# A two-block transformer kernel: order of work at the stage borders, more places for squares, weight loads exchanged, tiles joined

## The reference

```python
for l in range(DEPTH):                       # DEPTH = 2
    h = rms_norm(x, ln_mix[l])
    x = x + parallel_mixer(h, ...)           # grouped attention (g) beside latent attention (m), 8 heads each
    h = rms_norm(x, ln_mem[l])
    x = x + memory_cross_attention(h, rms_norm(mem, ln_mem_kv[l]), ...)
    h = rms_norm(x, ln_ffn[l])
    x = x + expert_choice_moe(h, ...)        # 16 experts, 64 tokens each, width 512
return rms_norm(x, ln_final)
```

```python
c_q  = rms_norm(q_lat, mla_q_norm);  q_m = (c_q @ w_q_b)
c_kv = rms_norm(kv_lat[..., :128], mla_kv_norm);  kv = (c_kv @ w_kv_b)
```

## Time and profile before

| | |
|---|---|
| median of three runs | 3210.32 us |
| the profiled execution | 3204.61 us |
| its span in the trace | 3202.8 us |
| PE busy | 2946.7 us (92%) |
| DVE, ACT, POOL busy | 1430.5, 1154.4, 264.8 us |
| mean DMA rate | 129 GB/s, in the expert stages 418 to 419 |
| mean granted clock of TensorE | 0.962 of full speed |

### The profile page before, as it was taken

The page is one execution under the profiler, slowest core; times in us unless marked ns, Lnnn a source line. Parts: engine busy times, 40 slices in busy tenths (PEclk is TensorE's granted clock), DMA queues, the critical chain, the costliest instruction groups (busy, mean ns, idle before and its releaser), DMA issues. The chain is left out here.

```text
span 3202.8 us, 41642 instructions
## 1 busy us (share of the span) xinstructions
PE 2946.7 (92%) x16852; PEld 2194.3 (69%) x16852; DVE 1430.5 (45%) x2193; ACT 1154.4 (36%) x1929; POOL 264.8 (8%) x350
## 2 busy tenths in 40 slices
PE   7999979978999899988999879999999899879998
PEld 5657855436668755446778658887887688658886
DVE  5665432246565423234544663322324553654444
ACT  4554421123654411143143542223223333543332
POOL 0011010000001200011012310000001012200000
PEclk9999989989999899989999989999999999989999
DMA  3011239961002379953332002323321132012221
GB/s 147 27 40 64 96 159 419 418 278 60 15 29 105 118 311 412 419 218 126 131 101 79 15 27 92 132 105 119 118 79 42 69 117 92 14 53 97 100 92 40
DMA packets 61356, 414.31 MB, mean 129 GB/s; under 512 B 6976, under 2 KB 7360, under 8 KB 13552
## 3 DMA queue, kind: packets, MB, share of 16 engines
q1 hardware_dynamic: 55520, 392.59, 31.4%
q0 software_dynamic: 4496, 16.98, 1.7%
q10 hardware_dynamic: 1152, 2.10, 0.2%
HBM read 409.53 MB, written 2.10 MB: 129 GB/s over the span
## 5 line engine op out<-in xcount | busy, mean ns | idle before, releaser
L1533 ACT ACTIVATE arena<-banks 128x512 f32<-128x512 f32 (+4 forms) x522 | 291.2, 561 | 933.8 <-PE banks L785 811.8
L785 PE MATMUL banks<-weight,arena 128*64 128x512 f32 (+5 forms) x2264 | 464.1, 570 | 44.6 <-ACT arena L1533 18.1
L785 PE MATMUL banks<-hidden,weight_part 128*128 128x512 f32 (+1 forms) x2304 | 446.3, 355 | 0.0
L785 PE MATMUL banks<-tokens_high,weight_part 128*128 128x512 f32 (+1 forms) x1536 | 420.5, 359 | 22.4 <-DVE tokens_low L2183 22.1
L785 PEld LDWEIGHTS banks<-hidden,weight_part 128*128 128x128 f32 x2304 | 381.0, 189 | 70.3 <-DVE arena L2183 3.5
L2287 DVE TENSOR_TENSOR weight_part<-weight,weight_part 128x2048 fp32r<-128x2048 f32 x124 | 285.4, 2305 | 224.1 <-ACT weight_part L1533 223.9
L1533 ACT ACTIVATE weight_part<-weight 128x2048 fp32r<-128x2048 f32 x124 | 236.6, 1909 | 370.7 <-PE banks L785 348.6
L785 PEld LDWEIGHTS banks<-weight,arena 128*64 128x64 f32 (+2 forms) x2264 | 165.1, 135 | 294.7 <-issue 251.6
L785 PEld LDWEIGHTS banks<-tokens_high,weight_part 128*128 128x128 f32 x1536 | 276.5, 191 | 81.3 <-DVE tokens_low L2183 28.7
L785 PE MATMUL banks<-tokens_low,weight_part 128*128 128x512 f32 (+1 forms) x768 | 274.6, 358 | 0.0
L2926 POOL TENSOR_TENSOR arena<-arena 128x512 f32<-128x512 f32 x72 | 88.7, 1232 | 1889.3 <-ACT arena L1533 1039.9
(11 more groups left out here) (217 smaller groups left out, 4137.5 us busy)
## 6 DMA issues: line engine op xcount, KB each, us to landing
weight<-in_w_gate SPq DMA_DIRECT2D x64, 1024.0 KB, 13.6
weight<-in_w_up SPq DMA_DIRECT2D x64, 1024.0 KB, 8.1
weight<-in_w_down SPq DMA_DIRECT2D x64, 1024.0 KB, 11.3
weight<-in_w_ff SPq DMA_DIRECT2D x64, 1024.0 KB, 4.8
weight<-in_ada_w SPq DMA_DIRECT2D x48, 1024.0 KB, 6.6
weight<-in_w_in SPq DMA_DIRECT2D x28, 1024.0 KB, 4.8
weight<-in_w_o SPq DMA_DIRECT2D x8, 1024.0 KB, 4.8
weight<-in_w_mem_kv SPq DMA_DIRECT2D x8, 1024.0 KB, 4.8
```

What stands on the lines that cost most here:

```text
L785: mm = lambda o, a, b, first=True, last=True: eng.matmul(o, a, b, start=first, stop=last, skip_group_check=True)
L1533: act = lambda o, i, f=ACT.Copy, **k: eng.activation(o, i, f, **k)
```

## The change

1. **Mixer, both layers.** The projections ckv and kr and both small norms' sums move from ahead of the attention into its turns 1 and 2. The four products for V of the latent branch move from turns 2 to 5 to turns 4 to 7, the splits of w_o two or three turns on.
2. **Squares.** For the entry of the mixer of layer 1 and of the block, `SQW` gives eight places for squares that lie in tensors not in use then, and `SQC` eight for the context. The last scatter runs without sums between its tiles; `entry_sums` takes them behind it, POOL's part last but one.
3. **Order in the experts' last pair.** The split of the mixer's first weight goes ahead of the last expert outputs' rounding on ACT and DVE. In layer 1 three ada chunks stand before the scatter, three behind it, two behind the sums, and the context's sums (before: ahead of the scatter) are put around the turn of the ada rows.
4. **ada.** The stationary operand has 32 columns (two conditions and zeros) instead of 2, all four groups of rows are written, and ACT copies the whole bank once instead of two rows four times. In the feed-forward of layer 0 `ada_rows` goes one chunk earlier.
5. **Loads.** In the block of layer 0 the ada chunks go one to three places ahead in SP's list against w_sv, w_nq, w_nk and w_nv.
6. **Feed-forward.** The split of the first ff1 chunk moves to the end of the stage before. Its first two tiles are joined (`joint3`); in layer 0 two more token tiles follow, then the context's first two joined, then two more. DVE makes all eight h, then all eight low parts, instead of alternating.
7. **Block layer 1.** ACT's work for the context (`block_high`, `context_shift`) goes behind its copies of the uv tiles.

The core of the diff:

```diff
@@ loads of block layer 0
             cols("w_u", 1024)
+            conditioned(1, AHEAD, AHEAD + 1)
             cols("w_sv", 1280)
-            conditioned(1, AHEAD, AHEAD + 3)
+            conditioned(1, AHEAD + 1, AHEAD + 4)
             outs(0)
-            conditioned(1, AHEAD + 3, KD)
+            conditioned(1, AHEAD + 4, KD)
+            conditioned(2, 0, 1)
             cols("w_nq", 256)
-            conditioned(2, 0, 2)
+            conditioned(2, 1, 3)
             cols("w_nk", 512)
...
@@ PE, ada
-                    i = mm(o[32 * g:32 * g + 2, :], CS[:, k, :], w[:, 512 * g:512 * g + 512], k == 0, k == KD - 1)
+                    i = mm(o[32 * g:32 * g + 32, :], CS[:, k, :], w[:, 512 * g:512 * g + 512], k == 0, k == KD - 1)
@@ PE, end of the experts
                 if l:
-                    norm_sums(("n1c", 0), NS, range(KD), KD, "one1024", CT)
+                    for k in range(3):
+                        ada(0, 0, k, PO)
                 scatter(PAIRS - 1)
-                norm_sums(nxt, NS, range(KD - 2, KD), KD, "one1024")
+                if l:
+                    for k in range(3, 6):
+                        ada(0, 0, k, PO)
+                entry_sums(nxt, NS)
@@ PE, entry of the block
-                    for k in range(KD):
+                    for k in range(6, KD):
                         ada(0, 0, k, PO)
+                    norm_sums(("n1c", 0), S, range(2), KD, "one1024", CT)
                     ada_turn(0, 0, PB)
+                    norm_sums(("n1c", 0), S, range(2, KD), KD, "one1024", CT)
@@ PE, turns of the mixer's attention
+                    if i == 1:
+                        norm_sums(("cq", l), S, range(2), 2, "one256")
+                        w = wcur[0] = weight_parts(("w_in", l, 4))
+                        tile3(("ckv", l), halves(w, 0), HP)
+                    if i == 2:
+                        norm_sums(("ckv", l), S, range(1), 1, "one128")
+                        tile3(("kr", l), halves(wcur[0], 1), HP, free=(WF(("w_in", l, 4)),))
@@ PE, first ff1 chunks
+                        if i == 0:
+                            first = wh, wl
+                            joint3([("f1", l, 0, m) for m in ms], [halves(first, m) for m in ms], XP, ...)
+                            continue
+                        for m in ms:
+                            tile3(("f1", l, 0, m), halves((wh, wl), m % 2), XP, ...)
+                        if both:
+                            joint3([("f1c", l, 0, m) for m in range(2)], [halves(first, m) for m in range(2)], CP, ...)
@@ ACT
+                if not both:
+                    block_high(l, S, 1)
+                    context_shift(l, S)
...
-                for g in range(4):
-                    act(AD[32 * g:32 * g + 2, :], ring.get(("ada", l, q))[32 * g:32 * g + 2, :]).then_inc(...)
+                act(AD, ring.get(("ada", l, q))).then_inc(*done(("ad", l, q), ring.free(("ada", l, q))))
@@ DVE, mod_norm
-                        if n == 2 and k >= 2:
-                            eng.wait_ge(*after(("hh", tag, k - 2)))
-                            stt(parts["HL"][:, k - 2, cols], H[:, k - 2, cols], ...)
+                    for k in range(KD if n == 2 else 0):
+                        eng.wait_ge(*after(("hh", tag, k)))
+                        stt(parts["HL"][:, k, cols], H[:, k, cols], ...)
```

More of the change, by code:

```diff
@@ L600, in build @@
             b = dict(H=(Carve(0) if l else c)(KD, T), HNH=c.rounded(f"rows_high{l}", TB, D))
+            b["SQW"] = Ring(st, "SQW" + t, [Carve(c.at - (KD - k) * T)(T) for k in range(KD)])
             low_at = c.at
@@ L1510, in _ @@
                                       [(S["HH"][:, k, cols], S["HL"][:, k, cols]) for k in range(KD)], N,
-                                      free=(WF(key),) if m % 2 and part == parts[-1][0] else (),
-                                      needs=[("h2", (tag, l), k) for k in range(KD)] if (s, m) == (0, 0) else ())
+                                      free=(WF(key),) if m % 2 and part == parts[-1][0] else ())
                     else:
@@ L1667, in _ @@
                 squares(("cq", l), S, [PB.get(("cq", l, j)) for j in range(2)])
-                eng.wait_ge(*after(("out", ("ckv", l))))
-                squares(("ckv", l), S, [PB.get(("ckv", l))])
-                root(("cq", l), S)
-                root(("ckv", l), S)
                 high(4)
-                copy(S["KR"][64:128, :], ("kr", l), PB.get(("kr", l))[64:128, :], ("krc", l))
                 def mla_prep(h):
@@ L1695, in mix_between @@
                 def mix_between(i):
-                    if 2 <= i < 2 + TB:
-                        copy(S["VM"][:, i - 2, :], ("vm", l, i - 2), PB.get(("vm", l, i - 2)))
+                    if i == 1:
+                        root(("cq", l), S)
+                        eng.wait_ge(*after(("out", ("ckv", l))))
+                        squares(("ckv", l), S, [PB.get(("ckv", l))])
+                    if i == 2:
+                        root(("ckv", l), S)
+                        copy(S["KR"][64:128, :], ("kr", l), PB.get(("kr", l))[64:128, :], ("krc", l))
+                    if VM_AT <= i < VM_AT + TB:
+                        copy(S["VM"][:, i - VM_AT, :], ("vm", l, i - VM_AT), PB.get(("vm", l, i - VM_AT)))
                     if i in PREP_AT:
@@ L1819, in _ @@
                         eng.wait_ge(*after(("scattered", l, p - 1)))
+                    if p == PAIRS - 1 and l == 0:
+                        split_high(("w_in", 1, 0))
+                    if p == PAIRS - 1 and l:
+                        for other in meet("block2"):
+                            eng.wait_ge(*other)
+                        eng.wait_ge(*after(("ctx",)))
+                        squares(("n1c", 0), B["four", 0], [C[:, k, :] for k in range(KD)], n=CT)
                     for ch in range(2):
@@ L1830, in _ @@
                 exp_set()
-                if l == 0:
-                    split_high(("w_in", 1, 0))
                 S4 = B["four", 0]
                 if l:
-                    for other in meet("block2"):
-                        eng.wait_ge(*other)
-                    eng.wait_ge(*after(("ctx",)))
-                    squares(("n1c", 0), S4, [C[:, k, :] for k in range(KD)], n=CT)
                     eng.wait_ge(*after(("final_scale",)))
@@ L2375, in mix_between @@
                 def mix_between(i):
+                    if i == 1:
+                        apply(("cq", l), S, [PB.get(("cq", l, j)) for j in range(2)], [S["CQ"][:, j, :] for j in range(2)], lambda k: v1("mla_q", l, k),
+                              lambda k: (("cqn", l),) if k else (), frees=[(PB.free(("cq", l, j)),) for j in range(2)])
+                    if i == 2:
+                        apply(("ckv", l), S, [PB.get(("ckv", l))], [S["CKV"]], lambda k: v1("mla_kv", l), lambda k: (("ckvn", l),),
+                              frees=[(PB.free(("ckv", l)),)])
+                    if i == 4:
+                        eng.wait_ge(*after(("krc", l)))
+                        tt(S["TBB"][R, :], K[E, :], S["TAB"][E, 3, :], MUL).then_inc(*done())
+                        tt(K[R, :], K[R, :], S["TAB"][R, 2, :], MUL).then_inc(*done())
+                        eng.wait_ge(vector_step, done.count)
+                        tt(K[R, :], K[R, :], S["TBB"][R, :], ADD).then_inc(*done(("ks", l)))
+                        eng.wait_ge(vector_step, done.count)
                     if i - 1 in PREP_AT:
@@ L2495, in expert_low @@
                 def expert_low(p):
+                    if p == PAIRS - 1 and l == 0:
+                        split_low(("w_in", 1, 0))
                     for ch in range(2):
```

199 lines of the change are left out of this document (108 added, 91 removed).

## The result

The changed kernel takes 3132.25 us at the median of four runs (3127.12 to 3141.26) against 3210.96 (3210.0 to 3211.62, four runs): the medians lie 78.7 us apart; by the ratio, 0.9765 with a 95% interval of 0.9751 to 0.9778, it is some 2.4% faster. The forecast was 3129 in a range of 3104 to 3164. Run again later, the same kernel gave 3137.32 at the median of four (ratio 0.9777, 0.9763 to 0.9790): executions of one program lie up to 14 us apart here (3127.12 to 3141.26), and that spread has a part in what follows.

A forecast was written before the change was run, and what follows sets the result against it. PE was taken as the bound, busy 2946.7 of 3202.8 us, with the whole effect in its pauses at stage borders. The terms summed to -81.0: 3204.6 becomes 3123.6, the median 3210.3 about 3129 us, range 3104 to 3164.

The forecast's parts named there:

- Mixer's entry: Attention entry, both mixers: projections cover the softmax wait of 7.16 us; -6.7 us each, -13.4 together.
- Entry of mixer 1: End of the experts, layer 0: split ahead of last rounding lets POOL start earlier; -9.6 us, bounds -6 to -10.5.
- Entry of the block: End of layer 1's experts to uv: ada chunks replace context sums before the scatter; -16.5 us, bounds -8 to -20.
- Loads: Beside gate and neighbourhood projections: exchanged loads remove PE's ada waits and slow rows; -15.4 us, bounds -6 to -19.
- no ada wait over 1 beside the projections: Sign expected in the profile after: PE waits at most 1 us for ada loads beside the projections.
- First feed-forward tiles: Feed-forward start, layer 0: PE resumes 4.3 us earlier, new stall of about 3.1 later; -8.5 us, bounds 0 to -11.
- Layer 1: Feed-forward start in layer 1, the same without context: PE resumes at 2832.5, not 2836.87; -5.2 us.
- ada_rows one chunk earlier: Feed-forward: the copy no longer stands before the next split, removing a 4.63 us wait and slow rows; -6.8 us.
- Block layer 1: Block entry, layer 1: copies ahead of ACT's context work cut PE's 4.94 us wait to 1.3; -5.6 us.
- 32 columns: Ada's 48 chunks: four filled column groups run beside each other, so widening from two columns costs 0.
- serial rival: Ada's 32-column chunks don't overlap and take 3.5 us each: +118 us, 3247 us in all; chance 0.04.
- The rival by which these stages swallow what is gained ahead of them: Expert stages are bound by their load stream and lose both mixers' 6.7 and the 9.6: 3152 us; chance 0.09.

The follow-up runs named there:

- u_attn: Changed kernel with the entry of the mixer's attention as before (ckv, kr and small norms ahead of the scores): 3145.54 us, ratio 0.9798.
- second traces: Kernel before and changed kernel each executed and traced once more, nothing edited: 3206.28 us (one run) and 3137.32 us.
- u_split: Changed kernel with only the split of the second mixer's first weight back behind the last rounding: 3140.17 us, ratio 0.9786.
- u_sq: Changed kernel with both entries' squares in the old ring of few places: 3137.54 us, ratio 0.9782.
- u_ada: Changed kernel with all eight first ada chunks behind the token norm's sums at the block's entry, as before: 3138.25 us, ratio 0.9778.
- u_loads: Changed kernel with SP's load order for the block of layer 0 as before: 3147.74 us, ratio 0.9812.
- nv_first: ff_relu with the load of w_nv one place earlier, ahead of one ada chunk: 3129.74 us, ratio 0.9753.
- ff_early: Changed kernel with the third ff1 chunk split ahead of the first hidden tiles in layer 0's feed-forward: 3135.68 us, ratio 0.9767.
- ff_relu: ff_early, with ACT also reading the token halves of the first two tiles early, freeing their banks: 3131.69 us, second time 3128.57 us.

## Why the prediction was right, and where its sizes were off

*Mixer's entry.* Right in kind and total: -13.4 forecast; -7.7 and -6.1 in the first traces, -7.4 and -7.9 in the second, and u_attn gives them back. The bank wait set at 0.7 measured 0.84; for the 1.7 of the first exponentials the rows show no wait. The row at 114.81 that the forecast calls turn 2's score is turn 3's, which its sum doesn't touch.

*Entry of mixer 1.* -9.6 forecast, -9.9 measured (-8.9 in the second traces); the root stands 9.3 us behind the scatter's start, 9.5 forecast. Its text names only the split, and counts DVE's 2.29 of it. By u_split the split's place is 5.7, since DVE had also stood 2.48 us for ACT's half; the squares' places are 2.1 (u_sq). What is left, some 2 us, belongs to the scatter without sums between its tiles; no run takes that back alone.

*Entry of the block.* -16.5 forecast up to uv; from the last low part to uv it was -17.2 in the first traces and -14.7 in the second. The table's row ends later, and its second pair shows only -12.0, as the 24 products of uv took 8.1 us there and not 5.4. The ada chunks in the scatter's shadow are some 4 of it (u_ada); the context's sums behind it were not taken back alone.

*Loads.* -16.4 with the copy of the rows; -14.2 and -1.0 behind it, -15.2, and u_loads gives 14.0 to 14.3 back. The new stall that was set at 2.5, a bank that waits for w_nv's split, is there with 2.23; with the one exchange that was tried it turned into an ada wait of its size (nv_first). The sign "no ada wait over 1 beside the projections" was missed by little: one of 1.44 us is left, 1.12 in the second trace.

*First feed-forward tiles.* The step that was mis-sized, in layer 0: -8.0 net forecast, -5.4 in the first traces, -4.7 in the second. It is not the resumption: from the last stall of the differential stage to PE's resumption it was 31.6 us and became 28.0 and 27.5, -3.7 to -4.1 where 4.3 less 0.5 for the moved split was forecast. Behind the resumption the forecast wanted 4.2 more, and there were 0.6 to 1.8 (62.8 to 61.0 and 62.1). The brackets that went, 3.1 us together, were replaced by the stall that had been counted with 3.1 and measured 3.17; the slow rows behind the new stall had not been counted: PE's busy time in this part is 57.8 and 58.9 us, and 56.3 in ff_relu, where the stall is 0.9. ff_early and ff_relu show what made the stall: the third chunk's split stood behind the first hidden tiles on ACT, and once it was moved, the order in which ACT reads the banks. With both seen to, the stretch is 84.6 to 84.8, 9.5 to 9.9 under before's. Layer 1: -4.7 forecast, -4.6 and -4.0 measured.

*ada_rows one chunk earlier*: -6.8, measured -6.5 (394.7 to 388.2 us over the chunks in which it lies). *Block layer 1*: -5.6, measured -6.8 and 1.2 more on the way to the gate stage. In the rows the first bracket is gone and the second is down from 4.94 to 1.15, but no run takes either part back alone. *32 columns*: 0, measured 1.06 against 1.04 for a chunk and 7.07 against 7.05 for eight; the serial rival is out. That four 128x32 tiles operate independently, as the Trainium skill, TensorEngine Tiling (Array Packing), Tiling Modes, has it, is borne out by these rows.

*What had no term.* The differential stage of layer 0, +4.7 in the first traces and +0.3 in the second, mostly the clock's level. The expert stages: in layer 0 +2.5, and the twelve traces of kernels with the change have 254.8 to 257.6 (mean 256.5), two of before 254.9 and 254.7; PE's waits for w_up are 12.2 us and not 8.4. In layer 1 the +2.0 of the first trace is spread: the twelve have 254.3 to 257.0 (mean 255.5), before 255.0 and 255.3. The rival by which these stages swallow what is gained ahead of them would have given 254.9 back in u_attn and more loss in layer 1; it gave 255.8 and no such loss. What makes the first stage some 2 us longer stays open.

*Idle and busy.* The forecast put nearly all of its 81 us into idle time (256 to near 180) and almost nothing into busy time. Measured are 51 us of idle and 20 of busy time. Its own terms had 13 us of slow rows in them (2.0 at each mixer, 5.1 beside the loads, 2.2 and 2.0 later), so that its sign for the busy time didn't fit its sum; on the idle side it had left out waits that came anew, 3.8 us more for w_up and 2.2 behind branch_low among them.

The sum of -81.0 came out as -71.3 between the first two traces and -66.6 between the second, and as -78.7 and -73.3 between the medians of the two timings: it was too large by 2 to 14 us, each time in the same direction. The trace of before on which it was built was a short one (3204.6 and, again, 3206.3, where the medians of before are 3208 to 3211), and the forecast added the distance back. That 3129 came within 3 us of 3132 is in part luck, worth 5 us or more: the second timing of the same kernel gave 3137.

## What to carry to other kernels

At a stage border, write down per engine what stands ahead of the first instruction that the next stage needs. A split in two halves of 1.91 and 2.29 us, moved ahead of the instruction that all wait for, was worth 5.7 us, as the halves ran one after the other and slow rows followed. Products that need only loads (here the conditions') fill such borders, some 4 us here, and the limit is then the load's landing. When a stall is filled, look at what holds the next one: ACT's order of work, then the order in which it reads the banks, turned 3.2 us into 2.5, and both together left 0.9.

## What had not been expected of the hardware

One program's stage of many short waits took 125.8 us in one execution and 128.8 in another, at a granted clock of 0.95 and 0.91, and 127.2 to 132.0 us at 0.92 to 0.88 in kernels whose work there is the same but for one split on ACT. The lengths lie in steps of some 1.5 us. In the same way the stretch from the memory stage to the router took some 146.2, 147.5 or 150.5 us in traces of the same code. Differences of 3 us in one stretch of one trace therefore say nothing here without a second one, while stretches without waits agree to 0.01 us (the last 292 us of the second feed-forward: 291.94 or 291.95 in all fourteen traces).
